# Causal and top-k masks of two attention layers: from products on TensorE to additions on VectorE

## The reference

```
x = x + ab_layer(norm(x))      # first attention layer: 8 "DSA" heads and 8 "FOX" heads
x = x + mlp(norm(x))
x = x + c_layer(norm(x))       # third layer: 16 heads, three branches
x = x + mlp(norm(x))
x = diff_attention_layer(x)    # fifth layer
```

```
s = where(mask, q @ k.T * scale, -inf);  m = max(s);  e = exp(s - m);  p = e / sum(e)
o = p @ v
```

## Time and profile before

| what | value |
|---|---|
| median of 3 runs | 926.53 us (925.9 to 928.71) |
| profiled execution, its own time | 924.48 us |
| its span in the trace | 922.6 us |
| PE busy | 903.0 us, 98% |
| DVE busy | 648.8 us, 70% |
| ACT busy | 513.6 us, 56% |
| POOL busy | 128.3 us, 14% |
| granted TensorE clock | 1.00 of full speed |
| first layer's steps | about 87 to 122 us of the span |
| third layer's steps | about 379 to 447 us |

### The profile page before, as it was taken

How to read it: one execution, slowest core, us unless ns; L and a number is a source line. 1 busy time by engine, 2 the same in 40 slices (tenths; PEclk the granted TensorE clock), 3 DMA queues, 4 the chain that set the end, 5 groups by cost and what they waited for, 6 DMA issues and landing times. The chain is left out here.

```text
span 922.6 us, 14840 instructions
## 1 busy us (share of the span) xinstructions
PE 903.0 (98%) x4844; PEld 753.1 (82%) x4844; DVE 648.8 (70%) x1168; ACT 513.6 (56%) x1019; POOL 128.3 (14%) x181
## 2 busy tenths in 40 slices
PE   8999999999999999999999999999999899999998
PEld 7878788888888878898888888888887778878776
DVE  5768756666666679766577666666876878777775
ACT  6654546444544565565464444544656666666573
POOL 1310200000000010245210000000430400300301
PEclk9999999999999999999999999999999999999999
DMA  9645024665555556400346555555474445454531
GB/s 363 222 143 166 13 93 140 207 198 186 190 190 189 182 178 202 146 1 1 102 150 206 190 197 183 185 194 189 137 228 137 137 138 174 149 178 140 171 104 47
DMA packets 40521, 146.39 MB, mean 159 GB/s; under 512 B 4496, under 2 KB 4752, under 8 KB 40464
## 3 DMA queue, kind: packets, MB, share of 16 engines
q1 hardware_dynamic: 40176, 145.43, 47.8%
q10 hardware_dynamic: 288, 0.21, 0.1%
HBM read 144.57 MB, written 1.05 MB: 158 GB/s over the span
## 5 line engine op out<-in xcount | busy, mean ns | idle before, releaser
L450 DVE TENSOR_TENSOR wl<-raw,wh 128x1024 fp32r<-128x1024 f32 x270 | 331.8, 1233 | 139.9 <-ACT wh L445 135.4
L445 ACT ACTIVATE wh<-raw 128x1024 fp32r<-128x1024 f32 x270 | 284.5, 1057 | 160.3 <-PE acc L347 139.8
L345 PE MATMUL acc<-wh,xhl 128*128 128x512 f32 (+1 forms) x472 | 191.9, 407 | 0.9 <-DVE wl L450 0.9
L347 PE MATMUL acc<-wh,xhl 128*128 128x512 f32 (+1 forms) x472 | 184.3, 390 | 0.0
L346 PE MATMUL acc<-wl,xhl 128*128 128x512 f32 (+1 forms) x472 | 183.9, 390 | 0.0
L345 PEld LDWEIGHTS acc<-wh,xhl 128*128 128x128 f32 x472 | 88.7, 188 | 24.4 <-issue 6.2
L347 PEld LDWEIGHTS acc<-wh,xhl 128*128 128x128 f32 x472 | 88.6, 188 | 19.3
L346 PEld LDWEIGHTS acc<-wl,xhl 128*128 128x128 f32 x472 | 88.8, 188 | 17.3 <-issue 1.0
L347 PE MATMUL acc<-wh,hl 128*128 128x512 f32 x256 | 100.4, 392 | 0.0
L346 PE MATMUL acc<-wl,hh 128*128 128x512 f32 x256 | 100.4, 392 | 0.0
L345 PE MATMUL acc<-wh,hh 128*128 128x512 f32 x256 | 100.2, 391 | 0.0
(11 more groups left out here) (313 smaller groups left out, 1328.3 us busy)
## 6 DMA issues: line engine op xcount, KB each, us to landing
raw<-stream SPq DMA_DIRECT2D x270, 512.0 KB, 3.4
h<-x SPq DMA_DIRECT2D x2, 512.0 KB, 4.8
out<-h SPq DMA_DIRECT2D x4, 256.0 KB, 2.1
row<-rows SPq DMA_DIRECT2D x1, 700.0 KB, 11.7
probs<-sel SPq DMA_DIRECT2D x1, 512.0 KB, 10.4
cst<-consts SPq DMA_DIRECT2D x1, 507.0 KB, 9.7
col<-cols ACTq DMA_DIRECT2D x1, 138.5 KB, 5.5
cst<-consts ACTq DMA_DIRECT2D x1, 64.0 KB, 4.4
```

The lines of the kernel that those rows point to most:

```text
L345: nc.tensor.matmul(out_, ah, bh, start=start, stop=False, skip_group_check=True)
L347: return nc.tensor.matmul(out_, al, bh, start=False, stop=stop_, skip_group_check=True)
L445: nc.scalar.activation(wh[:, u % SPLIT, :], raw[:, u % RAW, :], ACT.Copy).then_inc(w_hi, 1)
L450: nc.vector.tensor_tensor(wl[:, u % SPLIT, :], raw[:, u % RAW, :], wh[:, u % SPLIT, :].bitcast(F32), ALU.subtract).then_inc(w_lo, 1)
```

## The change

The mask products leave TensorE. VectorE does mask and maximum in one instruction, `tensor_tensor_reduce`: it reads the scores from PSUM and the mask from SBUF, writes -(score + mask) into `probs`, and its running minimum into `nb`. In the third layer there are four of these per step where there were two reductions. The exponentials then read and write `probs` in place, with scale -1. Since VectorE is now the one that first writes `probs[:, st % 2]`, it waits there for the transposes of step `st - 2` (`s_turned`), in place of ScalarE; and since ScalarE no longer reads PSUM, the scores of step `st` wait for the peaks of `st - 2` (`s_peaked`) and no longer for its exponentials. Two tiles and their copies on VectorE (`mskr`, `causr`) go.

```diff
             def ab_scores(st):
                 if st >= 2:
-                    pe.wait_ge(s_exped, 2 * (st - 1))
-                if st == FOX:
-                    pe.wait_ge(picked_set, 1)
+                    pe.wait_ge(s_peaked, 2 * (st - 1))
...
-                for a in range(2):
-                    mm((pair, acc)[a][st % 2][:, 0:KEYS], idr[:, :], (causr if st < FOX else picked)[:, :],
-                       start=True, stop=False, skip_group_check=True)
-                    if st < FOX:
+                if st < FOX:
+                    for a in range(2):
                         for t in range(T):
-                            mm(ab_bank(st, a, t), selr[:, 2 * st + a, :], decay[:, 0:(t + 1) * P], start=False,
+                            mm(ab_bank(st, a, t), selr[:, 2 * st + a, :], decay[:, 0:(t + 1) * P], start=t == 0,
                                stop=False, skip_group_check=True)
...
                 st = STEPS_AB + n
                 if st >= 2:
-                    pe.wait_ge(s_exped, 2 * (st - 1))
+                    pe.wait_ge(s_peaked, 2 * (st - 1))
...
-                for t in range(T):
-                    causal(banks[t], t).then_inc(s_scored, 1)
+                    last.then_inc(s_scored, 1)
...
             def exponentials(st):
-                if st >= 2:
-                    act.wait_ge(s_turned, 2 * (st - 1))
...
-                        src = ab_bank(st, a, t) if st < STEPS_AB else c_bank(st, t)[:, a * n:(a + 1) * n]
-                        last = s_.activation(pb[:, c0:c0 + n], src, ACT.Exp,
+                        last = s_.activation(pb[:, c0:c0 + n], pb[:, c0:c0 + n], ACT.Exp, scale=-1.0,
                                              bias=nbs[:, a, t:t + 1], accum_out=sus[:, a, t:t + 1])
...
+            def masked_peak(st, a, t, src, mask):
+                n = (t + 1) * P
+                c0 = t * 2 * P + a * n
+                return v_.tensor_tensor_reduce(probs[:, st % 2, c0:c0 + n], src, mask[:, t * P:t * P + n], -1.0, 3.4e38,
+                                               ALU.add, ALU.min, c_stat(nb, st)[:, a, t:t + 1])
+
             def peaks(st):
+                dve.wait_ge(s_turned, 2 * (st - 1))
                 for t in range(T):
                     dve.wait_ge(s_scored, 2 * st + t + 1)
-                    v_.tensor_reduce(c_stat(nb, st)[:, :, t], c_bank(st, t).rearrange("p (a k) -> p a k", a=2),
-                                     AX.X, ALU.max, negate=True).then_inc(s_peaked, 1)
+                    n = (t + 1) * P
+                    for a in range(2):
+                        last = masked_peak(st, a, t, c_bank(st, t)[:, a * n:(a + 1) * n], caus)
+                    last.then_inc(s_peaked, 1)
 
             def ab_peaks(st):
+                if st >= 2:
+                    dve.wait_ge(s_turned, 2 * (st - 1))
+                if st == FOX:
+                    dve.wait_ge(picked_set, 1)
                 for a in range(2):
                     dve.wait_ge(s_scored, 2 * st + a + 1)
                     for t in range(T):
-                        last = v_.tensor_reduce(c_stat(nb, st)[:, a, t:t + 1], ab_bank(st, a, t), AX.X, ALU.max,
-                                                negate=True)
+                        last = masked_peak(st, a, t, ab_bank(st, a, t), caus if st < FOX else picked)
                     last.then_inc(s_peaked, 1)
...
-                    v_.tensor_copy(mskr[:, :, :], caus[:, 0:P].unsqueeze(1).broadcast_to([P, 2, P])).then_inc(masks_set, 1)
-                    v_.tensor_copy(causr[:, :], caus).then_inc(masks_set, 1)
```

More of the change, by code:

```diff
@@ L229, in program @@
         decay = sb("decay", [P, SEQ], F32R)
-        picked = sb("picked", [P, KEYS], F32R)
+        picked = sb("picked", [P, KEYS])
         idr = sb("idr", [P, P], F32R)
-        mskr = sb("mskr", [P, 2, P], F32R)
-        causr = sb("causr", [P, KEYS], F32R)
         hr = sb("hr", [P, 2, SEQ])
@@ L892, in idx_scores @@
                 last.then_inc(idx_scored, 1)
-            def scores(st, q, keys, bias):
-                if st >= 2:
-                    pe.wait_ge(s_exped, 2 * (st - 1))
-                banks = [c_bank(st, t).rearrange("p (a k) -> p a k", a=2) for t in range(T)]
-                for t in range(T):
-                    mm(banks[t], q[:, t * P:(t + 1) * P], keys[:, :, 0:(t + 1) * P],
-                       start=True, stop=False, skip_group_check=True)
[L902 to L908, removed]
             def turn_p(st, a):
@@ L945, in ab_scores @@
                         last = mm(ab_bank(st, a, t), QK[rows, q, t * P:(t + 1) * P], QK[rows, k, 0:(t + 1) * P],
-                                  start=False, stop=True, skip_group_check=True)
+                                  start=st >= FOX, stop=True, skip_group_check=True)
                         if t == T - 1:
@@ L1022, in between @@
                 if u == U_VB + 2:
-                    pe.wait_ge(masks_set, 3)
                     pe.wait_ge(sel_set, 1)
@@ L1121, in c_scores @@
                     for part in range(2):
-                        mm(banks[t], c_q(n)[:, 0, t * P:(t + 1) * P], c_keys(n % CG, part)[:, :, 0:(t + 1) * P],
-                           start=part == 0, stop=False, skip_group_check=True)
-                for t in range(T):
-                    causal(banks[t], t).then_inc(s_scored, 1)
+                        last = mm(banks[t], c_q(n)[:, 0, t * P:(t + 1) * P], c_keys(n % CG, part)[:, :, 0:(t + 1) * P],
+                                  start=part == 0, stop=part == 1, skip_group_check=True)
+                    last.then_inc(s_scored, 1)
             def c_values(n):
@@ L1192, in first_steps @@
                 if uu == 2:
-                    pe.wait_ge(masks_set, 2)
+                    pe.wait_ge(masks_set, 1)
                     pe.wait_ge(q_hi, 8)
```

## The result

The changed kernel took 932.34 us (median of 9 runs, 928.33 to 936.42); the kernel before, beside it, 925.74 us (9 runs, 923.78 to 928.71). The ratio is 1.0065, with a 95% interval of 1.0045 to 1.0085: about 6 us slower. The forecast was +1.4 us, to 927.9. The measured median lies 0.3 us above the upper end of the range given, 932.0, and on the slow side of the 2.8 us that were called no change, which had 24%. That it lies so close to the range is in part luck: the forecast stood on a median of three runs, 926.53 us, and counted from the 925.74 measured beside the changed kernel the range would have ended at 931.2. Two executions further down, one of the kernel before (1115 us) and one of e9 (1275 us), had a mean clock of only 0.75 and 0.65 and are left out of every median, line and ratio.

What follows compares the result with a forecast made beforehand. In many iterations a ring of transposes and copies through ScalarE and VectorE was taken to be as long as TensorE's work. First layer -0.2 and third +1.6 us, added to 926.53, gave 927.9 us; 8 in 10: 924.6 to 932.

Steps and rivals of the forecast that it cites:

- The ring: Both layers: transposes a=0, ScalarE's copy, transposes a=1, now masked peaks, VectorE's copy, then the next iteration; 3.56 us.
- plain iterations: Third layer: three of 3.03 us and two of 2.98 become 3.56, +2.75 us.
- the sixth: Third layer: a further plain iteration, already held by the ring at 3.71 us, becomes 3.56, -0.15 us.
- iteration 10: Third layer: VectorE brings 0.45 us of other work into it, so 4.00 instead of 3.81 us, +0.19.
- full iterations: Third layer: longer than the ring and bound by TensorE; only part of each 0.24 us comes out, together -0.76 us.
- the last wait: Third layer: the last wait of a mix, 0.73 us into its iteration, goes to 0.34, -0.39 us.
- The masked peaks: VectorE's combined mask and maximum, four per step: 1.12 us per step, bounded above by 1.45 with accumulator reads on top.
- Rival B: Accumulator reads of the masked peaks paid in full, +0.33 us per step: +4.9 us, 932.8 us; full or partly, chance 0.21.
- The handovers: Between engines in both layers: 0.15 us from copy to TensorE; transposes a=1 start 1.19 us after a=0.
- The sum of waits: Both changed layers together: first layer -0.2 us, third layer +1.6 us, total +1.4 us.
- Rival C: TensorE stays the bound at transposes a=1, so all mask products come out: -7.5 us, 919.0 us; chance 0.06.
- Rival D: Ring bound by peaks no slower than the reductions, full iterations give their whole 0.24 us: -1.0, 925.5 us; chance 0.09.

Runs made afterwards that it cites:

- e9: Changed kernel with VectorE's copy ahead of the masked peaks and zero products in two TensorE gaps, against the kernel before: median 924.12 us, ratio 0.9989.
- e6: Changed kernel with zero products in two TensorE gaps and in the gaps the ring leaves, against the kernel before: median 928.05 us, ratio 1.0022.
- e7: Changed kernel with VectorE's copy of the transposed probabilities moved ahead of the masked peaks, against the kernel before: median 923.79 us, ratio 0.9985.
- e3: Kernel before with two unused additions on VectorE that lengthen TensorE's gap at 97 us, against the kernel before: median 927.74 us, ratio 1.0020.
- e5: The change in the first layer alone, third layer as before, against the kernel before: median 928.39 us, ratio 1.0028.
- e2: Kernel before with zero products in two TensorE gaps (first and fifth layer), against the kernel before: median 924.29 us, ratio 0.9984.
- e10: Kernel before with VectorE's copy ahead of its maxima and zero products in two TensorE gaps, against the kernel before: median 923.13 us, ratio 0.9974.
- e8: Kernel before with VectorE's copy moved ahead of its maxima, masks still products on TensorE, against the kernel before: median 923.30 us, ratio 0.9981.

## Why the prediction was right and wrong

- **The ring: right, and tested from two sides.** In the third layer plain iterations were forecast at 3.56 us and are 3.53 to 3.59; the layer's steps, from the first scores to the last mix, take 68.90 us instead of 67.02, +1.88 against +1.6 forecast. The parts hold one by one: plain iterations +2.80 (+2.75 forecast), the sixth -0.14 (-0.15), iteration 10 +0.27 (+0.19), full iterations -0.69 (-0.76), the last wait -0.38 (-0.39). e6 filled the ring's gaps and its length stayed; e7 took the peaks out of the ring and the iterations fell to 2.86.
- **The masked peaks: right.** 1.12 us per step, as in the earlier trace rows, their accumulator reads hidden. Rival B was wrong in its mechanism although its time, 932.8, is the one nearest to the median: it added 4.9 us of accumulator reads where the clock added some 4. A forecast is not confirmed by a number alone. The rule on the drained pipeline, from "The DRAIN you can't avoid" in "VectorE: DVE Perf Modes" of the Trainium skill, would by the prediction's estimate have asked for 1.75 (its terms, 2 x 0.28 + 2 x 0.42 + 4 x 0.08, add up to 1.72). The rows disagree with that here too: masked peaks start 0.22 us apart and last 0.29. The same paragraph of the page adds that an operation which is not held starts earlier, which the prediction left out and the rows bear out.
- **The handovers: right, but for one term.** In the third layer transposes a=1 start 1.22 us behind a=0 (1.19 forecast). In the first layer they start 1.31 behind (108.82 - 107.51): the step "a DSA step's scores end at about 1.1" was mis-sized. The 64-row products now come straight behind the transposes and begin 0.46 us after them (107.97 - 107.51), where the full-array mask product began 0.27 after them. So the ring is 3.71 us there and not 3.56, 0.6 us more over four iterations. In e6, at full clock, the last transposes of the first layer come 0.2 us later than before, where -0.2 was forecast.
- **The sum of waits: right in kind, short in size.** +1.4 forecast, 2.2 by the lines at clock 1.00 and 2.0 by the span of e6. Of what is missing, the first layer's ring is 0.6 and the third layer 0.3; the first DSA iteration came 0.1 us earlier than forecast (102.22 in e6).
- **The missing term: the clock.** The prediction took the granted clock of 1.00, read from one profiled execution, as given for all runs of both kernels, and counted a wait at its own length. It had no line for what longer gaps do to TensorE's speed. That is worth the other 4 us or so: the changed kernel's mean clock is 0.991 against 0.997 to 0.998, and filling the gaps with zero products (e6) gave back 4 us while the iterations stayed as long as they were. It is also why "TensorE busy about 7 us less" did not come (1.1 us less). Which of the gaps start the dips of the third layer, if any do, is not shown. The first layer's gap went from 1.05 us to 1.80, which the prediction did not work out at all: it followed VectorE's chain to the gap's end and not TensorE's to its beginning, which comes 1.1 us earlier.
- **Rival C: wrong,** as e7 shows: the products' time does not come out even when the order on VectorE is changed as well; 1.1 us at most, and not 7.5. The sign that was to refute the forecast, no brackets on TensorE, did not come.
- **Rival D: wrong** in its condition, since the masked peaks are slower than the third layer's reductions (1.12 against 0.94 us), and in its time.

## What to carry to other kernels

In this kernel, taking work off the busiest engine paid only where no ring through other engines was as long as its work; compare the ends of both in one iteration before counting the gain. When an instruction takes over the first write of a buffer, it takes over that buffer's wait too, and everything queued behind it waits along. Moving the copy ahead gave 2.2 us in the kernel before, at clock 1.00, without any change of the masks; the change of the masks on top gave 1.1 us at most. And look at the granted clock of every run, not of one: a gap on TensorE can cost more than its length.

## What the runs showed of the hardware that I had not expected

- A TensorE gap of 1.80 us (changed kernel) or 1.86 (e3) was followed by some 7 us at half speed in the profiled executions, one of 1.80 us in e5 by 3.4 us, and the same gap in e7 by none. In the profiled execution before, the one of 1.05 us at this place was followed by none. In e3 one run of twelve kept a mean clock of 1.00.
- The low level can last for 16 us in a stretch where TensorE is shown busy for all of the time (e9, 385 to 401 us). What ends it, and why the third layer is prone to dips also in kernels with its mask products (e2, e3, e5 and e10, between 401 and 412 us), is left open.
- An exponential from SBUF costs 0.04 to 0.05 us more than the same from PSUM: four take 1.76 us by their starts in e7 (390.33 to 392.09) and 1.59 in e8 (391.54 to 393.13). The Trainium skill has the same sign and size: the cycle table in "The TRN2 errata — SBUF-src ops pay a fixed extra latency per instruction" ("VectorE: DVE Perf Modes") has 224 fixed cycles for ScalarE from SBUF and 172 from PSUM; the difference of 52 is 0.043 us at its 1.2 GHz, an estimate from the page's figures. In the changed kernel's plain iterations no wait of TensorE was ended by an exponential, as forecast; in e7 the difference lengthens a full iteration by 0.15 us.
